# Feed-forwards with seven half products: rounding ahead of squares, hand-over bank by bank, weights in two landings, and the weight tiles' sums on VectorE

## What is computed

```python
def rmsnorm(x, g):
    xf = x.astype(jnp.float32)
    xf = xf * lax.rsqrt(jnp.mean(xf * xf, axis=-1, keepdims=True) + EPS)
    return (xf * g.astype(jnp.float32)).astype(x.dtype)

def swiglu_ffn(x, g, w_in, w_out):            # w_in 1024 x 5632, w_out 2816 x 1024
    h = rmsnorm(x, g) @ w_in
    gate, up = jnp.split(h, 2, axis=-1)
    return (jax.nn.silu(gate) * up) @ w_out

x = x + 0.5 * swiglu_ffn(x, lw['norm_ffn1'], lw['w_ffn1_in'], lw['w_ffn1_out'])
# ... projections, scan, sparse attention, memory attention ...
x = x + 0.5 * swiglu_ffn(x, lw['norm_ffn2'], lw['w_ffn2_in'], lw['w_ffn2_out'])
```

## Time and profile before

| | us |
|---|---|
| median of 3 runs | 3403.52 (3393.12 to 3404.36) |
| the profiled execution | 3407.41 |
| its span | 3405.5 |
| TensorE busy | 2919.5 (86%) |
| VectorE busy | 1555.5 (46%) |
| ScalarE busy | 972.5 (29%) |
| GpSimd busy | 426.4 (13%) |
| gate-up products (L712 to L714 with `ffn_gate_up`), busy | 573.5 + 562.4 + 563.8 |

### The profile page before, as it was taken

One profiled execution on the slowest core, in us unless ns is written; L12 is line 12 of the kernel. 1 busy time (PEld: TensorE's weight loads), 2 busy tenths in 40 slices (PEclk: granted clock), 3 DMA queues, 4 the chain that ended last, 5 costly groups with the idle time before them and its releaser, 6 DMA issues. The chain is left out here.

```text
span 3405.5 us, 49715 instructions
## 1 busy us (share of the span) xinstructions
PE 2919.5 (86%) x20104; PEld 2774.3 (81%) x20104; DVE 1555.5 (46%) x2766; ACT 972.5 (29%) x2021; POOL 426.4 (13%) x328
## 2 busy tenths in 40 slices
PE   4699999999899958996799995696475999998998
PEld 3699999999799947996799993496455999998997
DVE  3455565543351122342445552524436566565443
ACT  2233333311242222120434441412323333333211
POOL 3233333000000000000000000000015333230000
PEclk8799999999999976897569997798677999999999
DMA  2022212411234321211400004101200212214211
GB/s 81 31 69 73 74 64 73 166 64 64 80 52 50 126 100 58 66 38 41 121 7 13 1 1 127 52 25 38 72 26 32 73 65 73 77 61 157 90 64 53
DMA packets 103607, 221.36 MB, mean 65 GB/s; under 512 B 13684, under 2 KB 75156, under 8 KB 96276
## 3 DMA queue, kind: packets, MB, share of 16 engines
q1 hardware_dynamic: 98404, 207.88, 19.5%
q10 hardware_dynamic: 4976, 10.31, 0.8%
HBM read 172.85 MB, written 49.36 MB: 65 GB/s over the span
## 5 line engine op out<-in xcount | busy, mean ns | idle before, releaser
L712 PE MATMUL ffn_gate_up<-ffn_h_hi,ffn_w 128*128 128x272 f32 x1912 | 573.5, 300 | 183.2 <-DVE ffn_h_lo L832 66.5
L714 PE MATMUL ffn_gate_up<-ffn_h_hi,ffn_w 128*128 128x272 f32 x1912 | 563.8, 295 | 0.0
L713 PE MATMUL ffn_gate_up<-ffn_h_lo,ffn_w 128*128 128x272 f32 x1912 | 562.4, 294 | 0.0
L712 PEld LDWEIGHTS ffn_gate_up<-ffn_h_hi,ffn_w 128*128 128x128 f32 x1912 | 370.8, 194 | 203.7 <-issue 92.3
L713 PEld LDWEIGHTS ffn_gate_up<-ffn_h_lo,ffn_w 128*128 128x128 f32 x1912 | 371.7, 194 | 0.0
L714 PEld LDWEIGHTS ffn_gate_up<-ffn_h_hi,ffn_w 128*128 128x128 f32 x1912 | 371.1, 194 | 0.0
L837 DVE TENSOR_TENSOR ffn_w<-ffn_w_raw,ffn_w 128x512 fp32r<-128x512 f32 x264 | 224.1, 852 | 170.5 <-ACT ffn_w L603 165.9
L984 DVE SCALAR_TENSOR_TENSOR x<-ffn_down,x 128x364 f32<-128x364 f32 (+1 forms) x240 | 126.5, 535 | 328.5 <-PE ffn_down L309 328.5
L603 ACT ACTIVATE ffn_w<-ffn_w_raw 128x512 fp32r<-128x512 f32 x264 | 155.4, 623 | 152.3 <-DMA ffn_w_raw<-in_w_ffn_in 80.6
L1390 PE MATMUL ssd_hid_ps<-ssd_pages,ssd_cmp_w 128*128 128x128 f32 (+1 forms) x1280 | 171.3, 298 | 0.0
L307 PE MATMUL mix_ps<-h_mix_hi,mix_w_hi 128*128 128x364 f32 x480 | 161.6, 337 | 9.0 <-issue 6.0
(11 more groups left out here) (473 smaller groups left out, 6865.3 us busy)
## 6 DMA issues: line engine op xcount, KB each, us to landing
ffn_w_raw<-in_w_ffn_in SPq DMA_DIRECT2D x44, 1024.0 KB, 5.6
scratch_ffn_act<-ffn_prod SPq DMA_DIRECT2D x88, 272.0 KB, 2.7
ffn_h_raw<-scratch_ffn_act SPq DMA_DIRECT2D x44, 544.0 KB, 6.8
mix_w_raw<-in_w_mix SPq DMA_DIRECT2D x20, 512.0 KB, 3.6
ffn_h_raw<-in_w_ffn_out SPq DMA_DIRECT2D x16, 512.0 KB, 9.3
ssd_pages<-in_cmp_pages SPq DMA_DIRECT2D x64, 128.0 KB, 2.1
sn_slc_pages<-in_slc_pages SPq DMA_DIRECT2D x64, 128.0 KB, 2.1
ffn_w_sum<-in_w_ffn_out SPq DMA_DIRECT2D x14, 512.0 KB, 11.1
```

Of the source, the lines that this page charges most:

```text
L712: pe.matmul(out, hi, x_hi, start=start, stop=False, skip_group_check=chained)
L713: pe.matmul(out, hi, x_lo, start=False, stop=False, skip_group_check=chained)
L714: mm = pe.matmul(out, lo, x_hi, start=False, stop=stop, skip_group_check=chained)
```

## The change

It touches `ffn_stage` alone, for both feed-forwards.

1. ScalarE rounds the operand of pair j before it squares for pair j (`round_h(j)`, then `square(j)`). The last two pairs' squares go to other places (`squares_of`), so that they don't wait for the sums before; a square is now two instructions of half the size, each with its own count. Sums of a unit's last pair stand inside that pair's products. The first root (`root(0)`) waits until all of unit 0's products are done.
2. In units 0 and 1 TensorE takes the products in other orders: as the weights come, as banks come free (first pair of unit 1, each product waiting for its own step of `first_unit`), upper banks first (last pair of a unit). `first_unit` adds M6, M7, M5 first, then M2, M4, M3; unit 1 writes into `b12`, so that it doesn't wait for the store of unit 0.
3. The order of weight blocks is A11, A12, S1, S3, S2, S4, A22. A raw tile is loaded in two DMAs, blocks 0 and 2, then 1 and 3; the first goes out once S3's rest and the five sums of the tile before are made, the second after all rests. `round_w` and `combine` wait for the landing they need.
4. From weight tile 1 on VectorE makes the five sums (`combine(f, n)`, n = 0 to 4), between its other steps; GpSimd makes those of tile 0 alone. S2 of a tile is rounded in the even unit.
5. M1 of unit u waits for the first half of `ffn_prod` only, M2 for c11 of unit u - 2.

The core of the diff:

```diff
@@ -329,11 +329,14 @@
-A11, A12, S2, S1, S3, S4, A22 = range(7)
+A11, A12, S1, S3, S2, S4, A22 = range(7)
...
+AS_WEIGHTS_COME = ("M1", "M2", "M5", "M7", "M6", "M3", "M4")
+AS_BANKS_COME = ("M6", "M7", "M5", "M2", "M4", "M3", "M1")
+UPPER_BANKS_FIRST = ("M5", "M6", "M7", "M1", "M2", "M4", "M3")
...
+        def squares_of(j):
+
+            if j == PREPS - 1:
+                return [b12[:], sums[:, 1]]
+            return [sums[:, 1], by_halves(inv[:])[:, :, 1, :]] if j == PREPS - 2 else [sq[:, 0:2], sq[:, 2:4]]
...
@@ -485,10 +495,19 @@
-                def load_up(f):
-                    if f:
+                def load_up(f, half):
+
+                    if f and half == 0:
+                        sp.wait_ge(w_ready, N * (f - 1) + S3 + 1)
+                        sp.wait_ge(s_made, (N - 2) * f)
+                    elif f:
                         sp.wait_ge(w_ready, N * f)
-                    sp.dma_start(raw[:].rearrange("p b c -> p (b c)"), w_in[f]).then_inc(up_landed, 16)
+                    sp.dma_start(raw[:, half::2, :], w_in[f].rearrange("p (b c) -> p b c", b=4)[:, half::2, :]
+                                 ).then_inc((up_landed, up_rest_landed)[half], 16)
...
                 for u in range(2, U - 1):
-                    store(u - 2 if u == 2 else u - 1)
...
+                    if more:
+                        load_up(u // 2 + 1, 0)
+                    store(u - 1)
+                    if more:
+                        load_up(u // 2 + 1, 1)
@@ -583,9 +604,6 @@
                 for j in range(1, PREPS):
                     turn(j)
-                for f in range(1, FT):
-                    combine(f)
...
@@ -638,34 +664,36 @@
                 for j in range(1, PREPS):
+                    round_h(j)
+                    if j == K_PAIRS:
+                        first_copy(0)
+                        if not summed_before:
+                            root(0)
                     if not summed_before:
                         square(j)
-                        if j == PREPS - 1:
-                            root(1)
-                    round_h(j)
...
                     act.wait_ge(m_ready, made_at[u, "M1"])
-                    if u >= 4:
-                        act.wait_ge(prod_ready, 2 * (u - 1))
+                    act.wait_ge(prod_ready, 2 * (u - 1))
...
                     if u % 2 == 0:
+                        round_w(f, S2)
                         round_w(f, S4)
...
@@ -753,18 +796,24 @@
                     if m == "M1":
-                        if u < 4:
-                            pe.wait_ge(first_steps, 2 * N)
-                        else:
-                            pe.wait_ge(prod_ready, 2 * (u - 1))
+                        if u == 2:
+                            pe.wait_ge(first_m1, 2)
+                        elif u > 3:
+                            pe.wait_ge(prod_ready, 2 * (u - 1) - 1)
                         steps(p_bank, u, m, every, True, True).then_inc(m_ready, 1)
                     elif m == "M2":
+                        if u == 2:
+                            pe.wait_ge(first_steps, N + added["M2"])
+                        elif u > 3:
+                            pe.wait_ge(c11_done, u - 3)
...
                 scale_gate(0)
+                rest_w(1, A11)
+                combine(1, 0)
+                combine(1, 1)
+                first_unit(1, lambda: rest_w(1, A12))
+                combine(1, 2)
                 scale_twice(0)
                 multiply(0)
-                first_unit(1)
-                for a in (A11, A12, S2, S1, S3):
+                combine(1, 3)
+                for a in (S1, S3):
                     rest_w(1, a)
-                invert(1)
-                scale_gate(1)
+                combine(1, 4)
                 for u in range(2, U):
                     f = u // 2
                     more = u % 2 and f + 1 < FT
                     if more:
                         rest_w(f + 1, A11)
+                        combine(f + 1, 0)
+                        combine(f + 1, 1)
+                    if u % 2 == 0:
+                        rest_w(f, S2)
...
                     if more:
                         rest_w(f + 1, A12)
-                    if u > 2:
+                        combine(f + 1, 2)
+                    if u == 2:
+                        invert(1)
+                    else:
                         c12(u - 1)
-                        scale_gate(u - 1)
+                    scale_gate(u - 1)
...
                     if more:
-                        rest_w(f + 1, S2)
+                        combine(f + 1, 3)
                         rest_w(f + 1, S1)
...
                     if more:
                         rest_w(f + 1, S3)
+                        combine(f + 1, 4)
```

167 lines of the change are left out of this document (110 added, 57 removed).

## The result

The kernel after takes **3260.3 us** (median of 4 runs, 3253.21 to 3263.51), the one before took 3403.03 beside it (4 runs, 3393.12 to 3404.36): ratio 0.9584, 95% interval 0.9559 to 0.9608. The forecast was 3274, within 3256 to 3318. The profiled execution took 3263.51 us with a span of 3261.7; before they were 3407.41 and 3405.5. So 143.8 us of span went, where the sum had 129.8.

A forecast was written before the change was run, and what follows sets the result against it. TensorE, busy 86% of the span, was taken as the bound, each edit judged by which of its waits it ends. 54.9 + 5.9 + 69 = 129.8 off 3407.4 gave 3277.6, less 3.9 for the median: 3274 us, range 3256 to 3318.

The forecast's parts named there:

- Part 1: Units 0 and 1 of the first feed-forward: M7 of unit 2 starts at 87.9 instead of 142.82, 54.9 us gained.
- (a): First feed-forward, pair 1: rounding ahead of squares lets it start at 30.0 instead of 38.14.
- (b): First feed-forward, loop after pair 1: 35.6 us for six steps, as in the second feed-forward; pair 7's rest ends at 65.5.
- (c): First feed-forward, from the rest of pair 7 to M7 of unit 2: 22.0 plus 0.4, 22.4 us.
- Rival 2: Units 0 and 1: the clock stays low, 46 instead of 35.6 us and 3 in the transition; 3288 us, chance 0.11.
- Part 2: Units 0 and 1 of the second feed-forward: the transition to M7 of unit 2 shortens, 5.9 us gained.
- Part 3: Steady loop, 20 weight tiles in each feed-forward: pauses for `ffn_v` and `ffn_prod` end but for 0.1 us a tile, 69 us gained.
- keep 1.6 us: Steady loop: without GpSimd's silence speeding VectorE's instructions, each tile would keep 1.6 us of its pauses, 64 us in all.
- each us beyond costs 40 us: Steady loop: each us the second landing takes beyond 6.0 us after its issue costs 40 us in all.
- Rival 1: Steady loop: pauses stay because the odd unit waits for VectorE; 3343 us, half of it 3309; chance 0.18 with rival 4.
- Rival 3: Steady loop: the second landing comes late and VectorE holds c11 and all behind it; 204 us, 3478 us, chance 0.04.
- Rival 4: VectorE's fixed order leaves earlier landing and bank hand-over unused; half of Part 3, 3309 us; chance 0.18 with Rival 1.

The follow-up runs named there:

- the fixed order: Kernel after, without the hand-over by bank and with one order of products, M1 to M7, in the first two units: 3261.7 us.
- GpSimd's sums: Kernel after, with GpSimd making the five sums of every weight tile again, two landings kept: 3267.3 us.
- The late second half: Kernel after, with the request for a tile's second half held until ScalarE has copied M1 of the odd unit, 3.4 us later: 3340.8 us.
- the added 0.65 us: Kernel after, with one more VectorE operation once a tile ahead of c11 in the odd units: 3281.6 us.
- the kernel with one landing: Kernel after, with each tile loaded in one landing of 1024 KB after all seven rests of the tile before, VectorE's sums kept: 3344.2 us.
- both parts undone: Kernel after, with one landing per tile and GpSimd making the sums, rounding ahead of squares and hand-over by bank kept: 3300.8 us.

## Why the prediction was right, and where it was not

The sum was 54.9 + 5.9 + 69 = 129.8; the same places in the trace of after give 52.3 + 7.6 + 81.5 = 141.4, and 2.4 lie elsewhere, within what the code between the feed-forwards varies.

**Part 1, 54.9 said, 52.3 measured.** (a) Pair 1 was to start at 30.0 and did at 31.75. The first product of all came 0.84 later than before (16.07 for 15.22), so GpSimd's last step ended at 26.84 and not 25.9; the rest took 2.48 us for 2.14; and the products start 0.57 after it without idle time before them, since TensorE was still in sums of squares. (b) The loop's 35.6 us from the second feed-forward were close: the rest of pair 7 ended at 66.68, said 65.5, so 0.6 of the 1.75 came back. (c) The transition from there was to take 22.4 and took 23.8. ScalarE's root waits for the last sums (70.37), its copy of M1 comes at 71.97, and VectorE idles 2.02 us for the rounding behind it, so the sum's "plus 0.4 here because M1 of unit 1 is done only at 69" was too small in this trace. But that is clock: at 62 to 66 us it was granted 0.60. When the kernel after was run again it was 1.00 there, VectorE idled 0.50 us, and the transition took 22.3 us (66.20 to 88.49), as said. So of the missing 2.6 us some 1.4 are clock, and the rest is (a) less what (b) gave back. Rival 2 (low clock throughout) did not come: 1.00 from 50 to 58 us, and in every stretch from 16 to 62. Behind the 4.84 us wait before M6 the clock was at 0.50 once more (85 to 90 us), which cost nothing here, since M7 still waited 0.34 us for `ffn_v`.

**Part 2, 5.9 said, 7.6 measured.** In the second feed-forward, the rest of pair 7 ended at 2501.79, 47.60 us after the first product instead of 48.83, which I had credited with nothing, and M7 followed it by 21.7 (said 22.0, and 28.0 before). The 1.2 us before the rest of pair 7 are not the orders' either (47.61 with the fixed order); what made them is open. The zero for orders and hand-over is shown for this feed-forward (72.61 for 72.57); in the first up to 1.5 us may be theirs.

**Part 3, 69 said, 81.5 measured** (463.73 + 465.21 us for the 40 tiles before, 423.73 + 423.74 after). The mechanism was right to the instruction: rest of A11 at +0.96 (said 0.95), c11 at +3.09 (3.13), scaling at +5.30 (5.41), the copy ended at +7.00 (7.1), slack 0.22 (0.11). By their own figures the sum's terms make 69.6, not 69, and four were mis-sized. The allowance of 0.1 us a tile, 4 in all, was not needed: no tile pauses. A pause costs its idle time plus 0.23 and not 0.16; over 79 pauses 5.5 more. Two tiles of the second loop before, with pauses of 2.10 and 2.38 us, took 1.6 and 1.4 us beyond that, which the sum did not have. And the pauses inside the two loops were 60.2 us, not 61.0. Together 11.7 of the 11.9. The prediction's sign "M7 at 2528" took 37 us for the first loop, where half of 69 is 34.5; the loop gave 40.0, and M7 came at 2523.47. A reason beside the mechanism was wrong: GpSimd's work beside VectorE's was to "keep 1.6 us" of each tile, 64 us in all, if its slowing didn't end. With GpSimd's sums it goes on (rest of A12 1.40 us, ending 0.56 after GpSimd's sum) and the loop runs as fast, at 21.19. The Trainium skill, "SBUF — State Buffer", section "SBUF: two separate sides", has the lock of the port pair; these rows agree with it. What it costs depends on whether the chain has room. VectorE's own sums use that room up: 0.79 us with GpSimd's (6.84 - 6.05), 0.22 with its own.

**The landing.** It was put near 3.6 us and had 6.0 (5.87 by the rows, 344.63 to 350.50). DMA issues of the page (queue, count, KB each, median us to landing):

```profile
ffn_w_raw<-in_w_ffn_in SPq DMA_DIRECT2D x88, 512.0 KB, 4.1
```

4.1, 0.5 above the row it was taken from; the 11.1 of the earlier trace rows belong to a bunch of loads. Two requests of 512 KB cost the loop nothing against one of 1024: with them a tile takes 21.19 us in either kernel, which is TensorE's own time. The Trainium skill, "DMA: Bandwidth & Descriptors", section "Measured (HBM→SBUF, 128 partitions, SWDGE, issued from GpSimd)", gives its advice to batch to 1 MiB for the sake of a share of the peak bandwidth; the 84 us estimated from that page did not come here. The late second half shows that the sum's "each us beyond costs 40 us" is near: with S1 1.95 us late, less the slack of 0.22, that is 69, and it cost 77 (3340.8 - 3263.5), of which 3 are the restarts (0.07 each) and most of the rest a few tiles of 24 to 25 us.

**The rivals.** Rival 1 (VectorE becomes the bound) lies 0.22 us away: the added 0.65 us made it true at once. Rival 3 did not come (4.1 us for a landing). Rival 4, half of Part 3, fell; in its place stands that the loop needs nothing of the change but the two landings.

## What to carry to other kernels

When a pause recurs once per tile, look first at when the tile is asked for and which half of it is used first; here, two requests instead of one, each at the time its own space comes free, gave the whole loop in either kernel. Moving work off an engine that slows its neighbour helps only if the chain that is waited for gets shorter by it: count what the move puts ahead of the waited-for step, as well as what it frees. And where two engines serve one waiting third, put the step that is waited for ahead of the one that waits itself: rounding ahead of squares, one swap, was 39 us. And when a wait that is removed leaves the time where it was, look at the granted clock of the stretch before it: what ends last then can be the same work at the lower level.

## What the runs showed of the hardware

A pause can cost a second time. In the first loop of the kernel with one landing 16 tiles of 19 took 22.4 to 22.9 us, and three 25.1 to 25.2. Two stretches of it (length, busy us, PEclk, DMA share, GB/s), an ordinary tile and the piece in which a slow one pauses and goes on:

```profile
321.80:344.40 22.60, 21.41 (x170) 21.22 (x169) 14.50 (x26) 7.57 (x15) 0.00 (x0) 1.00 0.21 72
...
354.40:359.40 5.00, 5.00 (x30) 5.00 (x31) 4.03 (x8) 1.94 (x4) 0.00 (x0) 0.71 0.17 59
```

There, at its pause of 2.40 us (M7 at 354.35), TensorE was granted 0.71 over 5 us, a mean of its 1.2 GHz level (0.50) and 2.4 GHz, and the stretch holds 30 products where 5 us of an ordinary tile hold 42 at 1.00. The tile took 1.3 us more than its pause explains. In the loops of the kernel after no tile differs from 21.19 by more than 0.01 from the second on. The length of the pause alone doesn't decide: in the same loop a pause of 3.47 us was followed by 1.00 (103 to 108 us) and lost nothing, and with both parts undone one of 1.80 us lost 1.5 us (0.66 from 2551.8 to 2556.8). What does decide is not seen from these rows.

VectorE and GpSimd slow each other, but not in every instruction. Beside GpSimd's sums VectorE's rest of 512 columns took 1.40 us for 0.69 and its scaling 1.28 for 0.72, both of operands in SBUF; its addition c12 with an operand in PSUM kept its 0.42 (351.34, within a sum of GpSimd's from 350.94 to 352.55), in each of the 19 tiles between 100 and 500 us. In turn a sum of GpSimd's of 512 columns took 3.63 us beside VectorE's rest of 1,904 columns (at 13.51 in the kernel after), where the next one took 1.27.
